# Attention units split into scores and softmax, with statistics kept twice, in a hybrid encoder on one core

## The chip, the cores and the metric

The kernel runs on one core of one Trainium2 chip. The metric is the device time of one execution in microseconds (us), as the median of several runs. Engines are named as the profile names them: PE (TensorE; PEld its weight loads), DVE (VectorE), ACT (ScalarE), POOL (GpSimd), SP (SyncE, which here issues DMAs); ACTq and SPq are the DMA issues of ACT and SP.

## The reference

Two layers of an encoder over 512 prompt frames and 64 sample frames (576 rows of 1024), with a half-step SwiGLU FFN before and after a mixing block. All is fp32.

```python
def layer(h, ...):
    h = ffn_half(h, n1, w1g, w1u, w1d)           # h + 1/2 * (silu(x@wg) * (x@wu)) @ wd, D_FF 2816
    z = rmsnorm(h, nm) @ w_in                    # 1824 columns: u, va | q, k, v | cq, ckv, kpe
    m, st = token_mix(z, ...)
    h = h + m @ w_out
    return ffn_half(h, n2, w2g, w2u, w2d), st
```

token_mix has three parts. A: `u * (W_s v + b)` in chunks of 128. B: sliding-window attention, 8 query heads on 2 key heads of 64, over the own 64-frame chunk and the 128 frames before it, with a learned sink per head in the softmax. C: latent attention of 4 heads, scores from a 64-wide and a 32-wide part over all keys so far, softmax, values from a 128-wide latent. Both softmaxes are

```python
    m = jnp.maximum(jnp.max(s, axis=-1, keepdims=True), sk)      # C: without the sink sk
    p = jnp.exp(s - m)
    den = jnp.sum(p, axis=-1, keepdims=True) + jnp.exp(sk - m)
    return jnp.einsum('...hgqk,...khd->...qhgd', (p / den).astype(v.dtype), v)
```

Keys and values (B), latent and rotated key (C) and va of the sample are stored as further outputs.

## The kernel before

An fp32 product is made of three fp32r matmuls: every weight and activation is split in a high part (ACT) and a low part (POOL or DVE), and high*high, high*low and low*high are added in PSUM. Activations lie transposed, 128 channels by 576 frames, as two halves of 288. Per layer come the first FFN, the mixing phase, the rest of the output projection (c_part, L1745), and the second FFN. Each engine runs its own program; they meet in semaphores.

The mixing phase is written by one table, PLAN (L166), a list of steps. Every engine walks it in order and issues what it has to do for a step, so the table sets the order on all of them at once: PE in L1595, ACT in L1195, DVE in L2361. A step `name@p` uses PSUM pair p (two banks, `ps[p]`); there are four pairs, and PE waits before a step until the last step in its pair has been emptied (`evacuated`, L263, `tensor_needs`, L292). The steps:

- `w:x`: ACT splits weight slot x (w_high, L846), POOL makes its low part (w_low, L793); raw weights come by SP's DMAs, two raw buffers and a ring of four split slots. z:k and z:v have theirs before the phase.
- `z:x`: one input projection, 48 matmuls (L1384); DVE empties it with the norm's scale (L2409). `sumx`, `sumkv`, `sumq`: sums of squares, with a Sqrt on ACT.
- `sw:x`, `rot:x`: rotary embedding of k and q0 to q3: ACT issues four DMAs that copy z with its halves swapped (L1225) into z_swapped, and DVE multiplies and adds (L2450, L2454, L2457). For kpe and qp the swap is a matmul (`rot32`). The two z_swapped buffers alternate over k, q0, q1, q2, q3.
- `tw`, `tc`, `tk`, `tv`, `tva`, `tckv`, `tkpe`, `rkv`, `rep`: transposes and copies. `a`: part A. `qp`, `qn`, `kn`, `vc`: projections of part C. `A:m` (12 matmuls) and `B:m` (24): the output projection of parts A and B, column tile m, added to h by DVE (L2539). The projection of part C is c_part.
- Part B has ten units (five tiles of 128 frames, the last of 64, by two head pairs): `S:n` scores and softmax, `T:n` the turn (transposes of the probabilities, L1713, copied out by ACT to probsT), `O:n` the product with the values (L1721). Part C has ten: `MS:n`, `MT:n`, `MO:n` (L1736), for tiles 1, 3, 4, 2, 0 with 256, 512, 320, 384 and 128 keys. Window units have 128 keys (S:0, S:1), 256 (S:2 to S:7) or 192 (S:8, S:9).

A step S is, over the engines: PE scores (L1692; MS L1699, L1704); DVE fill of masked columns (L2487, L2491), maximum (L2494), neg_max (L2499) and sink_arg (L2503); ACT exponential of the sink (L1293) and of the scores with their sums (L1295; MS L1303); DVE den_all (L2506), reciprocal (L2515), division (L2522, L2524; MS L2526). All this stands in one place of DVE's order:

```python
                            emit(nc.vector.tensor_tensor(by_group(sink_arg)[0:nq], by_group(neg_max)[0:nq], unit_sinks(sinks, jj)[0:nq], ALU.add), names[n])
                            n += 1
                            adid(f"{step}.4")
                            emit(nc.vector.tensor_tensor(den_all[0:nq, :], den[0:nq, :], sink_exp[0:nq, :], ALU.add), names[n])
```

`adid` is DVE's wait for ACT. There is one tile of each statistic and one of probs; probsT has two.

SP (L671 to L765) loads the slots in their order; between the slots B1 and B2 it waits for tk.1, tv.1, tkpe.1, tva:1.1 and tckv.1 and issues nine stores. Behind the low part of slot C1 it loads the first set of the second FFN (set_raw, L607), which ACT splits at L1133.

Of the kernel before, what the change touches and what calls it, by code (L numbers as in the profile page):

```python
# [22 lines left out]
F32 = mybir.dt.float32  # L23
# [142 lines left out]
PLAN = """w:q0 z:k@0 sumx@3 w:q1 z:v@1 sw:k tw@2 w:q2 z:q0@0 rot:k z:q1@1 sw:q0 w:q3 w:va0 w:va1 sw:q1 tc@2 w:u0 rot:q0  # L166
z:q2@3 sw:q2 rot:q1 z:q3@1 rot:q2 sw:q3 w:u1 z:va0@0 tk@2 w:ckv w:cq0 rot:q3 z:va1@3 tva:0@0 S:0@2 z:u0@3 tv@1
tva:1@0 a:0@3 T:0@1 S:1@2 z:u1@0 w:cq1 O:0@1 w:cq2 T:1@2 S:2@0 z:ckv@3 T:2@2 w:kpe S:3@3 z:cq0@1 O:1@0 sumkv@3
T:3@1 S:4@2 O:2@3 a:1@1 z:cq1@0 w:qn T:4@3 S:5@1 O:3@2 z:cq2@0 O:4@3 T:5@1 S:6@2 z:kpe@0 sumq@3 tckv@1 O:5@0
T:6@3 w:A0 rkv@1 S:7@2 rep@1 qp@3 vc:0@0 rot:kpe@1 T:7@0 S:8@3 w:A1 qn:0@2 O:6@1 A:0@0 kn:0@3 T:8@2 S:9@1 O:7@0  # L170
A:2@2 qn:1@3 w:B0 A:1@1 rot:qp@0 T:9@2 tkpe@1 O:8@3 O:9@2 A:4@1 MS:0@2 vc:1@1 kn:1@3 w:B1 A:3@2 A:7@3 MT:0@0 w:B2
MS:1@1 B:0@0 A:6@3 MT:1@2 A:5@0 MS:2@3 MO:0@1 B:1@2 B:2@0 MT:2@1 MS:3@2 MO:2@1 B:3@0 MO:1@3 MT:3@2 w:B3 MS:4@1
B:4@3 MO:3@2 MT:4@1 MS:5@0 B:5@1 MT:5@2 MS:6@3 B:6@0 w:C0 MO:4@1 w:C1 MT:6@2 MS:7@3 B:7@1 MO:5@3 MT:7@2 MS:8@0
MO:6@2 MT:8@0 MS:9@2 MO:8@1 MO:7@0 MT:9@2 MO:9@0""".split()
# [35 lines left out]
def scalar_ops(step):  # L210

    kind, arg = split(step)
    n = {"z": 0, "sumx": 1, "sumkv": 2, "sumq": 4, "tw": 1, "tv": 2, "tc": 2, "tk": 2, "tva": 2,
         "rkv": 2, "tkpe": 2, "rep": 1, "a": 1, "kn": 1, "S": 5, "O": 1, "MS": 2, "MO": 1}.get(kind, 0)
# [12 lines left out]

def vector_ops(step):
# [25 lines left out]
PE_STEPS = [s for s in MIX if s not in SLOT_ENDS and s in PAIRS]  # L254
ACT_STEPS = [x for s in MIX for x in scalar_ops(s)]
# [7 lines left out]
def evacuated(step):  # L263

    kind, arg = split(step)
    if kind in ("z", "qp", "qn", "O", "MO", "A", "B"):
        return "vector", f"{step}.0"
    if kind in ("rot", "a", "tckv"):
        return "vector", f"{step}.1"
    return "scalar", scalar_ops(step)[-1]  # L270


def buffer_of(step):

    kind, arg = split(step)
    turn = [s for s in MIX if split(s)[0] in ("T", "MT")]
    return turn.index({"T": "T", "O": "T", "MT": "MT", "MO": "MT"}[kind] + f":{arg}") % 2
# [14 lines left out]
def tensor_needs(step):  # L292
# [4 lines left out]
    if prior is not None:  # L297
# [29 lines left out]
        "T": lambda: [vector_ops(f"S:{arg}")[-1]],  # L327
        "MT": lambda: [vector_ops(f"MS:{arg}")[-1]],
# [15 lines left out]
def build(nc, a, outs):  # L344
    ctx = ExitStack()
    with ctx:
# [31 lines left out]
        eps = sb("eps", [P, 2])  # L378
# [4 lines left out]
        neg_max = sb("neg_max", [P, 4])  # L383
        sink_arg = sb("sink_arg", [P, 4])
        sink_exp = sb("sink_exp", [P, 4])
        den = sb("den", [P, 4])
# [79 lines left out]
        zr = [at("z_swapped0", [P, NT], F32, pT0_at + 5120), at("z_swapped1", [P, NT], F32, temp0 + U)]  # L466
# [372 lines left out]
        def _(act):  # L839
# [355 lines left out]
            def mixing(layer):  # L1195
# [18 lines left out]
                for step in MIX:  # L1214
# [20 lines left out]
                    if kind == "z":  # L1235
# [12 lines left out]
                        continue  # L1248
                    if kind == "a":
# [38 lines left out]
                    elif kind == "S":  # L1288
                        i, jj, t0, nq, keys = swa_unit(arg)
                        W = sum(n for _, n in keys)  # L1290
                        first = len(vector_ops(step)) - 7
                        dve_did(act, layer, f"{step}.{first + 2}")
                        emit(nc.scalar.activation(sink_exp[0:nq, :], sink_arg[0:nq, :], ACT.Exp), f"{step}.0")  # L1293
                        for j in range(B_GROUP):
                            emit(nc.scalar.activation(probs[0:nq, j * 256:j * 256 + W], flat(p)[0:nq, j * 256:j * 256 + W],  # L1295
                                                      ACT.Exp, bias=neg_max[0:nq, j:j + 1], scale=B_SCALE,
                                                      accum_out=den[0:nq, j:j + 1]), f"{step}.{1 + j}")
                    elif kind == "MS":
                        i, pair, t0, nq, keys = mla_unit(arg)
                        W = sum(n for _, n in keys)  # L1300
                        dve_did(act, layer, f"{step}.{len(vector_ops(step)) - 3}")
                        for j in range(2):
                            emit(nc.scalar.activation(probs[0:nq, j * 512:j * 512 + W], flat(p)[0:nq, j * 512:j * 512 + W],  # L1303
                                                      ACT.Exp, bias=neg_max[0:nq, j:j + 1], scale=q_scale[0:nq, i:i + 1],
                                                      accum_out=den[0:nq, j:j + 1]), f"{step}.{j}")
# [67 lines left out]
        def _(pe):  # L1373
# [221 lines left out]
            def mixing(layer):  # L1595
                s = ZIN
                for step in MIX:
# [52 lines left out]
                    elif kind == "rot":  # L1650
                        src = {"kpe": kpe_rep, "qp": zs[1]}[arg]
                        if arg == "kpe":
# [172 lines left out]
        def _(dve):  # L1825
# [535 lines left out]
            def mixing(layer):  # L2361
# [22 lines left out]
                for step in MIX:  # L2384
# [8 lines left out]
                    if kind not in ("sumx", "sumkv", "sumq", "tw", "rot"):  # L2393
# [46 lines left out]
                    elif kind == "rot":  # L2440
# [6 lines left out]
                        else:  # L2447
                            adid("rep.0")
                            dve.wait_ge(mix_in, layer * N_MIX_IN + N_MIX_IN)
# [28 lines left out]
                    elif kind in ("S", "MS"):  # L2478
# [17 lines left out]
                        n += 1  # L2496
                        if swa:

                            emit(nc.vector.scalar_tensor_tensor(out=by_group(neg_max)[0:nq], in0=by_group(top)[0:nq], scalar=-B_SCALE,  # L2499
                                                                in1=unit_sinks(neg_sink, jj)[0:nq], op0=ALU.mult, op1=ALU.min), names[n])  # L2500
                            own(names[n])
                            n += 1
                            emit(nc.vector.tensor_tensor(by_group(sink_arg)[0:nq], by_group(neg_max)[0:nq], unit_sinks(sinks, jj)[0:nq], ALU.add), names[n])  # L2503
                            n += 1
                            adid(f"{step}.4")
                            emit(nc.vector.tensor_tensor(den_all[0:nq, :], den[0:nq, :], sink_exp[0:nq, :], ALU.add), names[n])  # L2506
# [134 lines left out]
```

## Time and profile before

| | |
|---|---|
| runs, median (lowest to highest) | 2100.07 us (2094.56 to 2100.23), 3 runs |
| span of the profiled execution | 2090.4 us; its own time is one of the kind above, 4.2 to 9.8 us over the span |
| busy, share of the span | PE 98%, PEld 95%, DVE 80%, ACT 47%, POOL 17% |
| mean granted TensorE clock | 0.994 |
| DMA | 178.35 MB, mean 85 GB/s |

The span runs from the first to the last instruction. The page's busy time of PE is modelled at its ends, so 98% does not mean that it works at its peak all that time. The views used below are the page, the busy time by windows, the waits of one engine (who released it and how long it had been idle), and the timeline (start, duration, instruction, and in brackets the idle time before it with its releaser). Times in the timeline are us from the span's start.

### The profile page before, as it was taken

To read this page: it belongs to the slowest core of one execution; us is meant where nothing else is said; L and a number is where in the kernel's file an instruction comes from. 1 tells how busy PE (TensorE), PEld (TensorE's weight loads), DVE (VectorE), ACT (ScalarE), POOL (GpSimd) and SP (SyncE) were. 2 spreads that over 40 slices of the span, in tenths; PEclk is the share of its full clock that TensorE was granted. 3 is DMA by queue.
4 is the path that set the end of the run, shared out by engine and by line. 5 is a ranking of instruction groups with operands and counts; after the bars stand their busy time and mean duration, and the time that the engine had idled before them with its cause. 6 is when DMAs were issued, how large, how long until landed. Compare 5 with 4: busy or idle time off the path is not lost. (4 is left out here: it accounts for less than half of the span.)

```text
span 2090.4 us, 41116 instructions
## 1 busy us (share of the span) xinstructions
PE 2048.2 (98%) x15435; PEld 1978.9 (95%) x15435; DVE 1681.3 (80%) x2481; ACT 977.5 (47%) x1772; POOL 359.9 (17%) x219
## 2 busy tenths in 40 slices
PE   9999999999999999999999999999999899999998
PEld 7999999999778999999989999999987699999998
DVE  5999998655655999998889999975565579999975
ACT  6544453324535544463465654533344464444532
POOL 0322200141110222200023222002402112222000
PEclk9999999999999999999999999999999999999999
DMA  4223323351111233232223322325312023332231
GB/s 131 94 88 100 96 75 105 94 128 42 46 41 62 86 95 100 91 92 85 77 82 101 100 80 87 103 76 128 94 45 64 31 62 101 100 93 85 83 105 64
DMA packets 236727, 178.35 MB, mean 85 GB/s; under 512 B 35808, under 2 KB 231616, under 8 KB 236608
## 3 DMA queue, kind: packets, MB, share of 16 engines
q1 hardware_dynamic: 231712, 170.36, 27.4%
q10 hardware_dynamic: 4896, 6.36, 1.1%
q8 instruction: 80, 1.31, 0.3%
q14 instruction: 39, 0.32, 0.1%
HBM read 170.12 MB, written 3.62 MB: 83 GB/s over the span
## 5 line engine op out<-in xcount | busy, mean ns | idle before, releaser
L1437 PE MATMUL pair<-t_parts,chunk_high 128*128 128x288 f32 x4592 | 919.2, 296 | 5.2 <-POOL chunk_low L799 2.5
L1437 PEld LDWEIGHTS pair<-t_parts,chunk_high 128*128 128x128 f32 x4592 | 738.9, 189 | 6.6 <-POOL chunk_low L799 3.2
L1437 PE MATMUL pair<-t_parts,chunk_low 128*128 128x288 f32 x2296 | 678.9, 296 | 0.0
L1437 PEld LDWEIGHTS pair<-t_parts,chunk_low 128*128 128x128 f32 x2296 | 432.7, 188 | 0.0
L799 POOL TENSOR_TENSOR chunk_low<-set_raw,chunk_high 128x512 fp32r<-128x512 f32 x164 | 237.5, 1458 | 871.5 <-ACT chunk_high L898 871.5
L898 ACT ACTIVATE chunk_high<-chunk_sum 128x512 fp32r<-128x512 f32 x328 | 203.9, 631 | 373.4 <-DVE chunk_sum L1990 190.3
L2002 DVE TENSOR_TENSOR chunk_low<-chunk_sum,chunk_high 128x512 fp32r<-128x512 f32 x328 | 214.4, 694 | 9.2 <-ACT chunk_high L898 1.9
L793 POOL TENSOR_TENSOR w_low<-raw,w_high 128x1024 fp32r<-128x1024 f32 (+2 forms) x48 | 115.0, 2402 | 619.6 <-ACT w_high L846 619.6
L1384 PE MATMUL pair<-hidden_high,w_high 128*128 128x288 f32 x896 | 192.1, 296 | 0.0
L1384 PE MATMUL pair<-hidden_high,w_low 128*128 128x288 f32 x896 | 191.9, 296 | 0.0
L1384 PE MATMUL pair<-hidden_low,w_high 128*128 128x288 f32 x896 | 191.6, 296 | 0.0
L846 ACT ACTIVATE w_high<-raw 128x896 fp32r<-128x896 f32 (+2 forms) x112 | 110.1, 984 | 140.5 <-PE pair L1570 56.0
L898 ACT ACTIVATE chunk_high<-set_raw 128x512 fp32r<-128x512 f32 x246 | 149.3, 620 | 0.0
L1384 PEld LDWEIGHTS pair<-hidden_low,w_high 128*128 128x128 f32 x896 | 144.5, 189 | 0.0
L1384 PEld LDWEIGHTS pair<-hidden_high,w_high 128*128 128x128 f32 x896 | 144.2, 189 | 0.0
L1384 PEld LDWEIGHTS pair<-hidden_high,w_low 128*128 128x128 f32 x896 | 144.2, 189 | 0.0
L1384 PE MATMUL pair<-x_high,w_high 128*128 128x288 f32 x480 | 105.1, 300 | 0.0
L1384 PE MATMUL pair<-x_high,w_low 128*128 128x288 f32 x480 | 102.7, 296 | 0.0
L1384 PE MATMUL pair<-x_low,w_high 128*128 128x288 f32 x480 | 102.6, 295 | 0.0
L1985 DVE TENSOR_TENSOR chunk_sum<-set_raw 128x512 f32<-128x512 f32 x82 | 82.4, 1005 | 14.9 <-PE pair L1437 14.5
L1021 ACT ACTIVATE chunk_high<-chunk_sum 128x512 fp32r<-128x512 f32 x64 | 39.1, 633 | 110.5 <-DVE chunk_sum L1910 95.2
L926 ACT ACTIVATE outputs<-outputs 128x576 f32<-128x576 f32 x88 | 59.4, 686 | 59.9 <-DVE outputs L2071 59.6
(300 smaller groups left out, 3732.6 us busy)
## 6 DMA issues: line engine op xcount, KB each, us to landing
set_raw<-in_w_up_dram SPq DMA_DIRECT2D x44, 1024.0 KB, 5.3
set_raw<-in_w_gate_dram SPq DMA_DIRECT2D x44, 1024.0 KB, 5.3
raw<-in_w_down_dram SPq DMA_DIRECT2D x64, 448.0 KB, 3.8
down_raw<-in_w_down_dram SPq DMA_DIRECT2D x16, 1024.0 KB, 5.4
raw<-in_w_in_dram SPq DMA_DIRECT2D x20, 512.0 KB, 4.0
raw<-in_w_in_dram SPq DMA_DIRECT2D x16, 256.0 KB, 3.8
raw<-in_w_out_dram SPq DMA_DIRECT2D x8, 512.0 KB, 3.5
raw<-in_w_out_dram SPq DMA_DIRECT2D x16, 256.0 KB, 4.0
```

The source lines that it names most:

```text
L793: nc.gpsimd.tensor_tensor(**low_of(s, slot_size(s))).then_inc(low_ready, 1)
L799: nc.gpsimd.tensor_tensor(out=cl[:, j], in0=set_raw[b][:, :, int(j == A12), 0:P], in1=ch[:, j].bitcast(F32), op=ALU.subtract).then_inc(low ...
L846: nc.scalar.activation(wh[s % RING][:, 0:n], raw[s % RAW][:, raw_from(s):raw_from(s) + n], ACT.Copy).then_inc(high_ready, 1)
L898: nc.scalar.activation(ch[:, j], src, ACT.Copy).then_inc(chunk_high, 1)
L926: nc.scalar.activation(g, g, ACT.Silu).then_inc(silu_done, 1)
L1021: nc.scalar.activation(ch[:, down_unit(g, j)], src, ACT.Copy).then_inc(d_high, 1)
L1384: mm = nc.tensor.matmul(ps[p][:, half, 0:HALF], w, x[:, half * HALF:(half + 1) * HALF], start=first and k == 0 and q == 0, stop=last and k ...
L1437: mm = nc.tensor.matmul(out, c[:, j, p, :], tr[p // 2][:, seat(p), x, t, :], start=p == 0 and n == 0, stop=p == KP - 1 and n == 2)
L1985: ins = nc.vector.tensor_tensor(cf[:, S1], block(b, 0, 1), block(b, 1, 1), ALU.add)
L2002: nc.vector.tensor_tensor(cl[:, j], src, ch[:, j].bitcast(F32), ALU.subtract).then_inc(low_by_dve, 1)
```

## The change

Each attention unit becomes two steps of the plan: S (or MS) is scores, fill, maximum, neg_max and sink_arg; E (or ME) is the exponentials on ACT and sum, reciprocal and division on DVE. The pair of S counts as emptied with the last exponential of E. neg_max, sink_arg, sink_exp and den exist twice and alternate over the units, so that S of the next unit may stand before E of this one; probs stays one tile, and E of a unit stands behind the turn of the unit before. The plan has a new order and other pairs for nearly all steps. `ex:n` is an exponential of one element on ACT; `ex:0` stands ahead of the first unit, `ex:1` near the end. The swapped halves of k, q1 and q3 go to sq_tmp in place of a piece of probsT. The wait for the tables of rot:kpe and rot:qp stands at whichever comes first. What each instruction computes is unchanged.

```diff
-MO:6@2 MT:8@0 MS:9@2 MO:8@1 MO:7@0 MT:9@2 MO:9@0""".split()
+MS:8@0 ex:1 MT:7@1 ME:8 B:5@3 MO:6@0 MO:7@1 MS:9@3 MT:8@0 ME:9 B:4@2 MT:9@3 w:C0 B:6@0 MO:8@2 MO:9@3 B:7@1 w:C1""".split()
...
+    if kind in ("S", "MS"):
+        return "scalar", scalar_ops(step.replace("S:", "E:"))[-1]
...
-        "T": lambda: [vector_ops(f"S:{arg}")[-1]],
-        "MT": lambda: [vector_ops(f"MS:{arg}")[-1]],
+        "T": lambda: [vector_ops(f"E:{arg}")[-1]],
+        "MT": lambda: [vector_ops(f"ME:{arg}")[-1]],
...
-        neg_max = sb("neg_max", [P, 4])
+        neg_maxs = sb("neg_max", [P, 2, 4])
+        neg_max = [neg_maxs[:, b, :] for b in range(2)]
...
-        zr = [at("z_swapped0", [P, NT], F32, pT0_at + 5120), at("z_swapped1", [P, NT], F32, temp0 + U)]
+        zr = [sq_tmp, at("z_swapped1", [P, NT], F32, temp0 + U)]
...
+                    if kind == "ex":
+                        emit(nc.scalar.activation(first_exp, eps[:, 0:1], ACT.Exp), f"{step}.0")
+                        continue
+                    if kind == "E":
+                        i, jj, t0, nq, keys = swa_unit(arg)
+                        W = sum(n for _, n in keys)
+                        b, sc = parity(step), flat(PAIRS[scores_of(step)])
+                        dve_did(act, layer, vector_end(scores_of(step)))
+                        emit(nc.scalar.activation(sink_exp[b][0:nq, :], sink_arg[b][0:nq, :], ACT.Exp), f"{step}.0")
+                        for j in range(B_GROUP):
+                            emit(nc.scalar.activation(probs[0:nq, j * 256:j * 256 + W], sc[0:nq, j * 256:j * 256 + W],
+                                                      ACT.Exp, bias=neg_max[b][0:nq, j:j + 1], scale=B_SCALE,
+                                                      accum_out=den[b][0:nq, j:j + 1]), f"{step}.{1 + j}")
+                        continue
...
+                    elif kind in ("E", "ME"):
+                        swa = kind == "E"
+                        i, jj, t0, nq, keys = (swa_unit if swa else mla_unit)(arg)
+                        heads, wide = (4, 256) if swa else (2, 512)
+                        W = sum(n for _, n in keys)
+                        b, n = parity(step), 0
+                        adid(scalar_ops(step)[-1])
+                        total = den[b]
```

How the plan moves instructions, at the places the prediction speaks of. Names in the rows as above; numbers behind a name are buffers; the changed kernel's lines lie some 30 lower (L1747 is the turn, L1770 MO, L1733 and L1738 the scores MS, L1418 a product).

PE, the last units of the mixing phase of layer 0, before:

```order
L1736 MATMUL pair<-probsT_102,vc_tok 64x64 x6
L1713 MATMUL pair<-ident,probs 128x128 x6
L1699 MATMUL pair<-k_nopeT_132,q_nopeT_134 128x128 x2
L1704 MATMUL pair<-kpeT,q_peT 128x128 x2
L1736 MATMUL pair<-probsT_101,vc_tok 64x128 x6
L1713 MATMUL pair<-ident,probs 128x128 x2
L1699 MATMUL pair<-k_nopeT_133,q_nopeT_135 128x128 x2
L1704 MATMUL pair<-kpeT,q_peT 128x128 x2
```

And of the change, from MO:6 to the first rows of the product B:4:

```order
L1770 MATMUL pair<-probsT_101,vc_tok 64x128 x6
L1770 MATMUL pair<-probsT_102,vc_tok 64x128 x6
L1733 MATMUL pair<-k_nopeT_132,q_nopeT_134 128x128 x2
L1738 MATMUL pair<-kpeT,q_peT 128x128 x2
L1747 MATMUL pair<-ident,probs 128x128 x2
L1418 MATMUL pair<-mixed_high,w_high_51 128x288 x2
L1418 MATMUL pair<-mixed_low,w_high_51 128x288 x2
```

Before, the scores of MS:9 follow the turn of MT:8, and MT:9 follows with two MO steps between. Now MS:9 stands ahead of MT:8, and the product B:4 (24 matmuls) between MT:8 and MT:9.

ACT, the beginning of the phase of layer 0, from the Sqrt of the norm to the weights va1, before:

```order
L1256 ACTIVATE rms<-pair,eps 128x576
L846 ACTIVATE w_high_54<-raw_50 128x1024
L1225 DMA z_swapped_123<-z_90 32x576 x4
L1206 ACTIVATE w_sT<-pair 128x512
L846 ACTIVATE w_high_51<-raw_49 128x1024
L1225 DMA z_swapped_124<-z_91 32x576 x4
L846 ACTIVATE w_high_52<-raw_50 128x1024
L846 ACTIVATE w_high_53<-raw_49 128x1024
L846 ACTIVATE w_high_54<-raw_50 128x1024
```

And of the change, to the swaps of q0 and q2:

```order
L1253 DMA sq_tmp<-z_90 32x576 x4
L874 ACTIVATE w_high_53<-raw_49 128x1024
L1234 ACTIVATE cache_kT_ckvT<-pair 128x384
L1234 ACTIVATE cache_kpeT<-pair 128x256
L874 ACTIVATE w_high_54<-raw_50 128x1024
L1253 DMA z_swapped_123<-z_91 32x576 x4
L1278 ACT_TABLE_LOAD
L1278 ACTIVATE eps<-eps 128x1
L1253 DMA z_swapped_123<-z_91 32x576 x4
```

The first row is the swap of q1; the swap of q0, which came ahead of it, now follows behind two weight splits and two copies, and the table load has come ahead of the first unit.

DVE, the last two units, of the change (E rows are RECIPROCAL and the division under it; L2577 adds a product to h, L2574 is mixed_low):

```order
L2553 RECIPROCAL inv_den<-den 128x2
L2564 TENSOR_TENSOR probs<-probs,inv_den 128x2x128
L2577 TENSOR_TENSOR h<-pair,h 128x576
L2574 TENSOR_TENSOR mixed_low<-pair,mixed_high 128x128 x2
L2522 MEMSET pair 64x2x64
L2529 TENSOR_REDUCE top<-pair 128x2
L2539 TENSOR_SCALAR neg_max<-top,neg_q_scale 128x2
L2553 RECIPROCAL inv_den<-den 128x2
```

Before, fill, maximum, neg_max, reciprocal and division of a unit followed each other with the wait for ACT between; here ME:8 is over, and B:5, MO:6 and MO:7 lie between it and the fill of MS:9, whose division follows as ME:9.

## Rows read from the trace of the kernel before

**Rows 1.** The page, busy time and share of PE and its weight loads.
```profile
PE 2048.2 (98%) x15435; PEld 1978.9 (95%) x15435; DVE 1681.3 (80%) x2481; ACT 977.5 (47%) x1772; POOL 359.9 (17%) x219
```
**Rows 2.** Windows: both mixing phases, stretch, busy us (count), PEclk, DMA share, GB/s.
```profile
411.00:644.70 233.70, 222.28 (x1740) 194.75 (x1738) 132.13 (x234) 95.73 (x240) 52.64 (x22) 0.98 0.27 69
...
1439.80:1672.40 232.60, 220.31 (x1739) 193.43 (x1738) 131.38 (x234) 95.74 (x240) 52.80 (x22) 1.00 0.27 69
...
637.60:647.90 10.30, 7.94 (x44) 6.34 (x44) 2.82 (x9) 2.36 (x9) 0.00 (x0) 0.50 0.01 2
1671.90:1675.30 3.40, 2.94 (x12) 2.97 (x13) 0.83 (x2) 0.00 (x0) 0.00 (x0) 0.50 0.02 5
```
**Rows 3.** Waits of PE over the span: total us, times, longest.
```profile
PE pair L1713 <- DVE probs L2526: 10.5, 10, 2.0
PE pair L1713 <- issue: 4.0, 6, 1.1
```
**Rows 4.** Timeline of PE, end of mixing in layer 0: start, us.
```profile
637.20 0.41 PE L1713 MATMUL pair<-ident,probs 128*128 128x128 f32 x2 [1.97 <-DVE probs L2526]
...
641.97 0.66 PE L1713 MATMUL pair<-ident,probs 128*128 128x128 f32 x2 [1.00 <-DVE probs L2526]
643.11 0.69 PE L1736 MATMUL pair<-probsT,vc_tok 128*64 128x128 f32 x4 [0.47 <-ACT probsT L1206]
644.70 0.58 PE L1384 MATMUL pair<-mixed_high,w_high 128*128 128x288 f32 x1 [0.89 <-DVE mixed_low L2536]
```
**Rows 5.** Timeline, window unit S:5 on DVE, a copy on ACT, the turn on PE.
```profile
518.24 0.27 DVE L2487 MEMSET pair<- 64x256 f32 x1
...
522.71 0.16 DVE L2506 TENSOR_TENSOR den_all<-den,sink_exp 128x4 f32<-128x4 f32 x1 [2.15 <-ACT probs L1295]
...
523.73 0.68 DVE L2524 TENSOR_TENSOR probs<-probs,inv_den 128x512 f32<-128x512 f32 x1
...
517.23 1.00 ACT L1206 ACTIVATE probsT<-pair 128x1024 f32<-128x1024 f32 x1
...
524.51 1.06 PE L1713 MATMUL pair<-ident,probs 128*128 128x128 f32 x8 [1.10 <-issue]
```
**Rows 6.** Timeline of DVE, latent unit MS:8, fill and division.
```profile
634.47 0.17 DVE L2487 MEMSET pair<- 64x128 f32 x1 [0.91 <-PE pair L1704]
...
636.67 0.42 DVE L2526 TENSOR_TENSOR probs<-probs,inv_den 128x256 f32<-128x256 f32 x1
```
**Rows 7.** Timeline of PE, the product z:va0 and two transposes behind it.
```profile
451.32 0.43 PE L1384 MATMUL pair<-x_high,w_high 128*128 128x288 f32 x2
...
457.73 0.27 PE L1664 MATMUL pair<-ident,kT 128*128 128x128 f32 x1
457.83 0.27 PE L1665 MATMUL pair<-ident,kT 128*64 128x128 f32 x1
```
**Rows 8.** Swaps: timeline of ACT's issues; DMA issues with KB and us to landing.
```profile
424.02 2.53 ACTq L1225 DMA_DIRECT2D z_swapped<-z  x4
...
z_swapped<-z ACTq DMA_DIRECT2D x40, 72.0 KB, 2.8
```
**Rows 9.** Timeline of DVE and POOL near the rotation of q0.
```profile
432.65 0.76 DVE L2450 TENSOR_TENSOR kT<-z,cos 128x576 f32<-128x576 f32 x1
...
438.25 0.76 DVE L2409 TENSOR_TENSOR z<-pair,rms 128x576 f32<-128x576 f32 x1 [3.31 <-PE pair L1384]
439.04 2.65 DVE L2450 TENSOR_TENSOR qT<-z,cos 128x576 f32<-128x576 f32 x1
...
436.33 4.75 POOL L793 TENSOR_TENSOR w_low<-raw,w_high 128x1024 fp32r<-128x1024 f32 x2 [5.73 <-ACT w_high L846]
```
**Rows 10.** The first set of the second FFN: SP's issue, ACT's split, landing.
```profile
629.87 0.37 SPq L607 DMA_DIRECT2D set_raw<-in_w_up_dram  x1
...
654.25 1.04 ACT L1133 ACTIVATE chunk_high<-set_raw 128x1024 fp32r<-128x1024 f32 x1
...
set_raw<-in_w_up_dram SPq DMA_DIRECT2D x44, 1024.0 KB, 5.3
```

More of the change, by code:

```diff
@@ L254, with scores_of, parity @@
 PE_STEPS = [s for s in MIX if s not in SLOT_ENDS and s in PAIRS]
+SCORES = [s for s in MIX if split(s)[0] in ("S", "MS")]
+EXPS = [s for s in MIX if split(s)[0] in ("E", "ME")]
+TURNS = [s for s in MIX if split(s)[0] in ("T", "MT")]
+VALUES = [s.replace("T:", "O:") for s in TURNS]
+assert [s.replace("S:", "T:") for s in SCORES] == TURNS == [s.replace("ME:", "MT:") if s[0] == "M" else s.replace("E:", "T:") for s in EXPS]
+for n in range(len(TURNS)):
+    assert MIX.index(SCORES[n]) < MIX.index(EXPS[n]) < MIX.index(TURNS[n]) < MIX.index(VALUES[n])
+    if n + 1 < len(TURNS):
+        assert MIX.index(TURNS[n]) < MIX.index(EXPS[n + 1])
+    if n + 2 < len(TURNS):
+        assert MIX.index(EXPS[n]) < MIX.index(SCORES[n + 2]) and MIX.index(VALUES[n]) < MIX.index(TURNS[n + 2])
+def scores_of(step):
+    return step.replace("E:", "S:")
+def parity(step):
+    return SCORES.index(scores_of(step)) % 2
 ACT_STEPS = [x for s in MIX for x in scalar_ops(s)]
@@ L275, in buffer_of @@
     kind, arg = split(step)
-    turn = [s for s in MIX if split(s)[0] in ("T", "MT")]
-    return turn.index({"T": "T", "O": "T", "MT": "MT", "MO": "MT"}[kind] + f":{arg}") % 2
+    return TURNS.index({"T": "T", "O": "T", "MT": "MT", "MO": "MT"}[kind] + f":{arg}") % 2
 def before_in_pair(step):
@@ L1248, in mixing @@
                         continue
+                    if kind == "ex":
[12 more added lines that the diff above has]
+                        continue
+                    if kind == "ME":
+                        i, pair, t0, nq, keys = mla_unit(arg)
+                        W = sum(n for _, n in keys)
+                        b, sc = parity(step), flat(PAIRS[scores_of(step)])
+                        dve_did(act, layer, vector_end(scores_of(step)))
+                        for j in range(2):
+                            emit(nc.scalar.activation(probs[0:nq, j * 512:j * 512 + W], sc[0:nq, j * 512:j * 512 + W],
+                                                      ACT.Exp, bias=neg_max[b][0:nq, j:j + 1], scale=q_scale[0:nq, i:i + 1],
+                                                      accum_out=den[b][0:nq, j:j + 1]), f"{step}.{j}")
+                        continue
                     if kind == "a":
@@ L1287, in mixing @@
                         copy(knT[arg][:, :], flat(p)[:, 0:KEYS], f"{step}.0")
[L1288 to L1305, printed above, removed]
                     elif kind in ("T", "MT"):
@@ L1651, in mixing @@
                         src = {"kpe": kpe_rep, "qp": zs[1]}[arg]
-                        if arg == "kpe":
+                        if step == min(("rot:kpe", "rot:qp"), key=MIX.index):
                             pe.wait_ge(mix_in, layer * N_MIX_IN + N_MIX_IN)
@@ L2392, in mixing @@
                         own(DVE_STEPS[emitted[0] - 1])
[L2393 removed]
+                    if kind not in ("sumx", "sumkv", "sumq", "tw", "rot", "E", "ME"):
                         pe_did(dve, layer, step)
@@ L2448, in mixing @@
                             adid("rep.0")
+                        if step == min(("rot:kpe", "rot:qp"), key=MIX.index):
                             dve.wait_ge(mix_in, layer * N_MIX_IN + N_MIX_IN)
```

60 lines of the change are left out of this document (30 added, 30 removed).

## The prediction

> **What bounds the kernel.** The page comes first. TensorE (PE) is busy 2048.2 us of 2090.4 [rows 1], so a change of order can win only where PE is idle or slow. The three runs lie 4.2 to 9.8 us above that span (median 2100.07); I take the change off the median, since what lies outside the span is not touched. About 0.3% (6 us) is what a measurement of this kernel can tell from no change.
>
> The windows over the two mixing phases say how much there is: in layer 0, from 411.0 to 644.7, PE is busy 222.28 of 233.70 us; in layer 1 220.31 of 232.60 [rows 2]. That is 11.4 and 12.3 us idle, 23.7 of the span's 42.2. PE's waits name the releasers: the largest is the turn of the probabilities (L1713), which waits for the division (DVE, L2526) or for "issue", 10.5 and 4.0 us in all [rows 3]. The timeline shows where: the last units of latent attention have nothing between scores and turn, so PE stands 1.97 and 1.00 us, then 0.47 and 0.89 us before the output projection [rows 4]. DVE (132 us busy of 234), ACT and POOL are far from full [rows 2]. The bound inside this phase is latency: a chain PE, DVE, ACT, DVE, PE per unit, with too little PE work laid over it.
>
> **The change, term by term.**
>
> 1. *Idle taken away.* Before, a unit's step S held scores, statistics, exponentials and division, in one place of every engine's order, and one set of statistics allowed one unit in flight. Now S is scores and maximum, E the rest, and S of the next unit may be issued before E of this one has ended. What counts is PE work between the end of a unit's scores and its turn. The chain it must cover, for a window-attention unit of 256 keys: first fill at 518.24, sums added at 522.71, division over at 524.41, turn at 524.51; with the hand-over to the fill 6.5 us [rows 5]. The shortest latent one, 128 keys, has fill at 634.47 and division over at 637.09, so 2.8 us [rows 6]; wider ones lie between the two, some 3.5 us for 256 keys and 4.7 for 384 (estimates: the fill's row and these two chains, by the number of keys). PE work is priced by rows: a product of 48 matmuls is 6.4 us, from 451.32 to 457.73 [rows 7], so one of 24 is 3.2 to 3.4 and one of 12 is 1.6 to 1.8. Laying the new plan out with those and the durations of the small steps, I get from scores to turn 7.7 us or more for units S:0 to S:5, 6.9 and 6.8 at the shortest of the later ones (S:6, S:9), and for latent units 4.2 (MS:0, 256 keys), 4.8 (MS:5, 320 keys), 7.4 (MS:6) and 3.8 (MS:9, 128 keys). The order at the end shows it: a product of 24 stands between the last scores and their turn, where nothing stood. All cover their chains, by 0.3 to 10 us.
>
> The second chain is from turn to turn, because there is still one probs tile: transposes 1.06, copy out 1.00, exponentials (DVE waits 2.15 for them), sum and division 522.71 to 524.41, 6.1 us with the hand-overs [rows 5]. The shortest new distance of two window turns is 6.7 to 6.9 us (T:5 to T:6, T:8 to T:9, the latter with 192 keys); of two latent ones 3.7 (MT:8 to MT:9), where the chain is about 2.6 (128 keys: transposes 0.41, and the rest of rows 4 and 6 in place of rows 5). So the idle goes: -11.4 and -12.3 = **-23.7 us**.
>
> 2. *Tails.* Each pause also costs the drain that the view counts as busy: one matmul's record is 0.27 us where the next starts 0.10 later when nothing stops it [rows 7]. With some 19 pauses a layer at about 0.13 us: **-5 us** for both layers.
>
> 3. *The clock.* In 637.6 to 647.9 PE ran at a granted 0.50, the 1.2 GHz level, and in 1671.9 to 1675.3 again, while all other stretches of the phases show 1.00; both begin within or just behind the pauses of the last units [rows 2, 4]. Work of 7.94 and 2.94 us busy there would take half: **-5.4 us**. The Trainium skill says the same of the cause ("TensorE: Matmul & The Clock Gate", the section on oscillation: pauses of PE bring the gate back to half), and the trace agrees with it; nothing in the sum uses the page.
>
> Ceiling: 23.7 + 5 + 5.4 = 34 us.
>
> 4. *Pauses that the new order makes.* (a) Swaps. ACT now issues q1's half-swap ahead of q0's, with two weight splits (1.05 us each) and the table copies between. Four issues take 2.5 us and data land 2.8 us after issue [rows 8]. z:q1 is scaled at about 27.9 us of the phase, so q1's swap is issued by 30.5, q0's by 35.9 and landed at 38.7; rot:q0 ends at 40.3, and only then does DVE empty pair 0 (z:q2), which PE wants at 40.3 for tv: 1 us. (b) POOL. A DVE instruction with two SBUF inputs that meets a w_low waits for it: at 439.04 it took 2.65 us beside POOL's two w_low from 436.33 to 441.08 (2.4 each), against 0.76 at 432.65 without them, while the one that reads PSUM at 438.25 took its 0.76 beside the same POOL work [rows 9]. The Trainium skill has the rule ("GPSIMD Engine Reference", Specifications: contention with VectorE instructions in a two-port mode or with two SBUF inputs), and it speaks against this change, which lays those instructions more densely under 22 w_low a layer. I find three meetings where the cover is under 1 us: rot:q3 before S:1 (0.5), neg_max of S:3 with kpe's split, before T:3 (0.6), division of ME:6 with B3's split, before MT:6 (0 or 1.4; I take 0.7). (c) PSUM pairs that are emptied 0.4 to 0.8 us before they are needed, some 15 of them: 0.2. Sum 3.0 a layer, **+6 us**. Below, this is 0; above, each of four meetings costs a full w_low, 2.4 us, 9.6 a layer, 19 in all. I take 6 since only divisions and rotations that start inside a w_low pay.
>
> 5. *Covered, priced at nothing.* The statistics kept twice add no instruction. The extra exponential of one element brings the Exp table load ahead of the first unit, on ACT alone, where T:0 is covered by 12.9 us of products [rows 7]. q0's swap buffer is now sq_tmp, free from the first mean to cq0. The key copy tk and tkpe come later, and SP waits for them before nine stores and B2's weights: tkpe is copied at about 162.7 us of the phase, ten issues at 0.37 and a landing of 5.3 make 171.7 [rows 10], and ACT splits B2 at 177. If that cover went, B:4 would wait microsecond for microsecond. The last weight set C1 is split only behind MO:9: then w_low (2.4) and SP's load of the next FFN's first set, issued at 629.87 before, 14.8 us ahead of the projection. Now it is issued 0.7 us behind the projection's start and lands 5.3 later, at +6.0; ACT takes it at 654.25, +9.6 from 644.70, or about +8.2 at full clock [rows 4, 10]. 2 us are left. The FFNs stay as they are, PE-bound.
>
> Sum: -34 + 6 = **-28 us**, 2072.
>
> **Rivals.** *No new pause of note* (15%): -32 to -36, about 2066. For it: all worked slacks are positive but four. *Port and swaps bind* (19%): by the skill's rule taken strictly, every two-SBUF instruction in those four places meets a w_low whole: -34 + 19 = -15, 2085. Against it: before, with 22 w_low a layer, DVE lost no PE time that the waits show other than through L2526. *The FFN's first set is late* (6%): should w_low C1 slip behind others by 4 us, the load lands at +10, 2 us late, 4 in both layers: 2076. *The change does not do what it says* (3%): a pair is still given back only at the last exponential, so early scores could find none free and PE would pause as before: 2100. Against it: pairs are spread so that S of the next unit has another one than E. *Slower* (5%): E makes DVE stand waiting for ACT (2.15 us for a unit [rows 5]) with the emptying of z and B products behind it in its order. If PE then waits for a pair at each of the 20 turns, it decides once a turn costs more than 0.85 us (34 / 40); at 1.2 us a turn it is -34 + 48 = +14, 2114. Against it: I find the pair in hand at 18 of 20 turns.
>
> **How the numbers follow.** The forecast 2072 has 52% (2068 to 2079). With the rivals, 2062 to 2086 holds over eight tenths: below by the ceiling, above by the four full meetings. Faster by over 0.3%: 52 + 15 + 19 + 6 and a little less for the unforeseen, 0.89; within 0.3%: 0.06; slower 0.05.
>
> **What would show it.** Right: PE idle in each mixing phase near 3 us; the turn's waits on DVE below 2 us in both layers together; a granted clock of 1.00 through the phase and the projection; the phase 217.7 + 3 = 221 us. Term 4 right: PE waits at tv or the scores of S:0 on a DVE z or qT, and at T:3 and MT:6 on the division. Wrong: idle above 7 us a layer, a wait on a PSUM pair at many turns, or a wait for chunk_high at the first FFN tile.

## The result, and the profile after

The changed kernel takes 2058.0 us (median of 4 runs, 2057.43 to 2061.27) against 2097.6 for the kernel before (4 runs, 2094.56 to 2100.23): ratio 0.9816, 95% interval 0.9803 to 0.9828. It is faster by 39.6 us where I had forecast 28 off a median of 2100, so the time lies 14 us under the forecast and 4 under the lower end of the range.

The profiled executions differ by less than the medians: 2090.4 us of span before, 2059.5 now, 30.9 apart. On the page PE is busy 16.7 us less and idle 14.2 us less:

```profile
span 2059.5 us, 41110 instructions
...
PE 2031.5 (99%) x15435; PEld 1975.0 (96%) x15435; DVE 1683.0 (82%) x2481; ACT 978.1 (47%) x1776; POOL 359.7 (17%) x219
```

The instructions are the same but for ACT's one-element exponentials, two a layer; 42.2 us of PE idle [rows 1] have become 28.0. The windows of both kernels over each mixing phase with the output projection behind it (a little longer than in [rows 2], so that the last pause is inside) show where. Columns as in [rows 2]; first the kernel before:

```profile
411.00:659.10 248.10, 236.68 (x1836) 209.15 (x1835) 142.63 (x250) 102.74 (x251) 52.83 (x23) 0.98 0.27 69
1439.80:1686.40 246.60, 234.31 (x1836) 207.43 (x1835) 141.71 (x250) 102.75 (x251) 52.92 (x23) 0.99 0.27 70
```

and the changed kernel, with its two stretches at the granted 0.5 at the end:

```profile
412.00:645.10 233.10, 229.28 (x1837) 208.04 (x1836) 144.00 (x250) 103.04 (x253) 53.29 (x23) 0.99 0.28 74
1424.30:1655.40 231.10, 229.12 (x1837) 208.19 (x1836) 142.03 (x250) 103.24 (x253) 53.30 (x23) 0.99 0.29 74
472.40:475.80 3.40, 3.40 (x23) 3.14 (x20) 2.98 (x8) 2.06 (x11) 0.00 (x0) 0.50 0.03 8
1551.00:1554.40 3.40, 3.40 (x17) 3.30 (x17) 2.74 (x9) 2.12 (x5) 0.00 (x0) 0.51 0.00 0
```

494.7 us have become 464.2, 30.5 less: that is the whole difference of the spans but 0.4. PE stands 3.8 and 2.0 us where it stood 11.4 and 12.3. Its waits over the span now have three entries from these phases; the 10.5 us on the division of [rows 3] are gone, and nothing of [rows 4] is left at the phase's end (the last turns and outputs have no idle time before them, and ACT takes the next FFN's first set at 640.22, with the projection still running until 645.1):

```profile
PE pair L1726 <- DVE qT L2492: 3.5, 2, 2.4
...
PE pair L1696 <- DVE z L2443: 1.4, 2, 0.9
...
PE pair L1747 <- issue: 0.9, 2, 0.4
```

These are the scores of S:1 (2.40 and 1.07 us in the two layers), tv (0.94, 0.48) and the turn T:3 (0.43 each). PE's timeline in layer 0, where L1696 is tv and L1726 is S:1:

```profile
453.44 0.74 PE L1696 MATMUL pair<-ident,vT 128*128 128x128 f32 x5 [0.94 <-DVE z L2443]
...
471.42 2.04 PE L1726 MATMUL pair<-kT,qT 64*128 64x128 f32 x24 [2.40 <-DVE qT L2492]
```

And what DVE did on the way there: the rotation of q1 waits 3.56 us for its swap (4 issues begun at 440.05) and then takes 2.79 and 2.83 us, beside two of POOL's w_low. The rotation of q0 (450.12) begins as soon as that is over, with no wait for its own swap, and the emptying of z:q2, for which tv waits, comes behind it. The rotation of q3 takes 2.02 for an operation of 0.76:

```profile
444.44 2.79 DVE L2489 SCALAR_TENSOR_TENSOR sq_tmp<-sq_tmp,eps,sin 128x576 f32<-128x576 f32 x1 [3.56 <-DMA sq_tmp<-z]
447.26 2.83 DVE L2492 TENSOR_TENSOR qT<-qT,sq_tmp 128x576 f32<-128x576 f32 x1
450.12 0.76 DVE L2485 TENSOR_TENSOR qT<-z,cos 128x576 f32<-128x576 f32 x1
450.80 0.81 DVE L2489 SCALAR_TENSOR_TENSOR z_swapped<-z_swapped,eps,sin 128x576 f32<-128x576 f32 x1
...
452.53 1.55 DVE L2443 TENSOR_TENSOR z<-pair,rms 128x576 f32<-128x576 f32 x2
...
467.73 2.02 DVE L2485 TENSOR_TENSOR qT<-z,cos 128x576 f32<-128x576 f32 x1
...
470.51 0.76 DVE L2492 TENSOR_TENSOR qT<-qT,sq_tmp 128x576 f32<-128x576 f32 x1
```

POOL at the same times, the two w_low of 444.20 together in one row:

```profile
444.20 5.27 POOL L821 TENSOR_TENSOR w_low<-raw,w_high 128x1024 fp32r<-128x1024 f32 x2 [7.36 <-ACT w_high L874]
...
466.66 2.48 POOL L821 TENSOR_TENSOR w_low<-raw,w_high 128x1024 fp32r<-128x1024 f32 x1 [4.79 <-ACT w_high L874]
```

So the pauses went as forecast, and from profile to profile the gain is 30.9 against 28 forecast; the terms below show that part of this agreement is luck. Left to explain: the 9 us by which the medians differ more than the profiles, what each part of the change is worth, and which cause stands behind the pauses that are left.

### The profile page after: what moved, and what is told of

Read it like the earlier page. It is cut to its first block and busy times, and to the rows that moved or that the text cites. A ratio compares the mean times of both kernels' runs of the same rounds, so it can differ in the third digit from the quotient of the medians.

```text
span 2059.5 us, 41110 instructions
## 1 busy us (share of the span) xinstructions
PE 2031.5 (99%) x15435; PEld 1975.0 (96%) x15435; DVE 1683.0 (82%) x2481; ACT 978.1 (47%) x1776; POOL 359.7 (17%) x219
## 5 line engine op out<-in xcount | busy, mean ns | idle before, releaser
L1418 PE MATMUL pair<-hidden_high,w_high 128*128 128x288 f32 x896 | 191.9, 296 | 0.0
L1418 PE MATMUL pair<-hidden_high,w_low 128*128 128x288 f32 x896 | 191.9, 296 | 0.0
L1418 PE MATMUL pair<-hidden_low,w_high 128*128 128x288 f32 x896 | 191.8, 296 | 0.0
L1418 PEld LDWEIGHTS pair<-hidden_low,w_high 128*128 128x128 f32 x896 | 144.5, 189 | 0.0
L1418 PEld LDWEIGHTS pair<-hidden_high,w_high 128*128 128x128 f32 x896 | 144.2, 189 | 0.0
L1418 PEld LDWEIGHTS pair<-hidden_high,w_low 128*128 128x128 f32 x896 | 144.2, 189 | 0.0
L1418 PE MATMUL pair<-x_high,w_high 128*128 128x288 f32 x480 | 105.3, 301 | 0.0
L1418 PE MATMUL pair<-x_high,w_low 128*128 128x288 f32 x480 | 102.9, 296 | 0.0
L1418 PE MATMUL pair<-x_low,w_high 128*128 128x288 f32 x480 | 102.8, 296 | 0.0
```

The lines of the kernel that those rows point to most:

```text
L1418: mm = nc.tensor.matmul(ps[p][:, half, 0:HALF], w, x[:, half * HALF:(half + 1) * HALF], start=first and k == 0 and q == 0, stop=last and k ...
```

## Experiments

Every kernel here was timed in five rounds beside the kernel before. For each profile the time of both phases with their projections is split into three parts: idle (from PE's gaps), clock (half of PE's busy time inside stretches at 0.5), and rest, which is what is then left above the 454.5 us of e9, the kernel without pauses.

**e1_before.** The kernel before again, unchanged.

> The kernel before, unchanged, to settle the base of the sum. The profiled execution had a span of 2090.4 us and, with the 1.8 us that lie outside the span in the runs of the changed kernel, would read 2092.2, below all four runs shown (2094.56 to 2100.23). Theory: the executions differ in how long TensorE stands at the half clock. Then the runs' spans follow their granted clocks, about 2.1 us of span for each 0.001 of mean clock, a second profile shows other half-clock stretches than 637.6 to 647.9 and 1671.9 to 1675.3, with the same pauses. Rival: the pauses themselves vary (DMA landings); then the clocks are equal and the idle time of PE differs from 42.2 us by the difference of the spans.

Measured: 2096.7 us (11 runs, 2092.71 to 2099.55), ratio to itself 0.9998 [0.9989, 1.0007]; the profiled run has 2095.1 us of span, 4.7 more than the first profile. The windows of this profile:

```profile
411.70:662.70 251.00, 239.35 (x1837) 211.25 (x1836) 143.18 (x250) 102.83 (x251) 53.10 (x23) 0.97 0.26 68
1441.80:1691.10 249.30, 237.94 (x1837) 210.23 (x1836) 141.98 (x250) 102.87 (x251) 52.95 (x23) 0.97 0.26 69
536.70:540.10 3.40, 3.11 (x14) 2.05 (x15) 1.97 (x7) 1.16 (x5) 0.00 (x0) 0.50 0.13 43
639.10:652.80 13.70, 10.99 (x55) 9.10 (x56) 4.11 (x12) 3.33 (x11) 0.00 (x0) 0.50 0.03 5
1567.50:1570.90 3.40, 3.40 (x18) 2.62 (x14) 1.82 (x6) 1.02 (x5) 0.00 (x0) 0.50 0.00 0
1669.90:1680.20 10.30, 7.94 (x44) 6.35 (x45) 2.87 (x10) 2.32 (x9) 0.00 (x0) 0.50 0.01 2
```

The idle time is the same (23.0 us against 23.7), the pauses stand at the same places, but 30.8 us of the phases ran at the half clock instead of 13.7: 12.7 us of cost against 5.4. These 7.3 more, with idle 0.7 and rest 1.0 less, are the 5.6 by which these phases are longer. Over the 50 executions of this kernel in these series, the seven with the highest mean clock (0.993 and 0.994) have spans of 2090.4 to 2091.9, the four with the lowest (0.985) 2097.8 to 2098.2; between them the order is loose (at 0.987 spans run from 2092.4 to 2095.9). The slope is about a fifth of the 2.1 us for 0.001 that I had put down (some 0.45 by a line through 32 of them). A likely reason is that the mean counts stretches in which little work was slowed: the changed kernel's at its start, 8.2 to 25.3, costs at most 0.3 us (412.0 us to the mixing phase, 411.7 in e5, which has none there). Between these two profiles the cause is the clock; the slope was wrong, and over all executions the mean clock tells the span only loosely. The first profile of before had clock 0.994 and 2090.4 us, the lower end of those seven.

**e2_old_order.** The changed code with the order of before.

```diff
-... S:0@1 E:0 z:va0@3 rot:q3 z:va1@0 w:u1 T:0@3 tva:0@1 S:1@2 S:2@3 E:1 ...
+... tva:0@0 S:0@2 E:0 z:u0@3 tv@1 tva:1@0 a:0@3 T:0@1 S:1@2 E:1 z:u1@0 ...
```

> The changed code with the order of before: every entry for a unit's softmax stands directly behind that for its scores, the entries for the Exp table load are left out, pairs and swaps as before. Theory (the gain is all from the order): statistics kept twice and the moved swap scratch cost and give nothing, 2097 us, ratio 0.998 to 1.002, and PE idle again 11 to 12 us in each mixing phase. Rival (the code gives or takes something by itself, such as the scratch in another place or the table load): off by over 3 us.

Measured: 2096.3 us, ratio 0.9994 [0.9985, 1.0003]; idle 11.6 and 11.2 us. The code alone (statistics twice, two entries a unit, the swap scratch in sq_tmp) gives and takes nothing that these runs can tell (0.1%, 2 us). The gain is in the order, with the pairs that belong to it.

**e3_not_ahead.** The changed kernel, one unit in flight.

```diff
-... S:1@2 S:2@3 E:1 tva:1@1 w:ckv z:u0@0 w:cq0 T:1@1 E:2 ...
+... S:1@2 E:1 tva:1@1 w:ckv z:u0@0 w:cq0 T:1@1 S:2@3 E:2 ...
```

> The changed kernel, but each unit's scores moved to directly before its softmax, behind the turn of the unit before: one unit in flight again; order of everything else, pairs and swaps as changed. Theory (half of the idle goes through scores ahead, half through more work laid between): by my layout of the order the cover falls below the chain at S:6 (2.2 of 6.5 us), S:7 (3.7), S:8 and S:9 (4.9), MS:1 (2.2), MS:3 (1.6) and MS:5 (2.6), about 12 us of pauses a layer: 2080 us. Rival (the new order of products alone does it, scores ahead is an ornament): 2058 to 2062. Second rival (without scores ahead the new order is worse than the old, since products stand between softmax and turn no better): 2095 or more.

Measured: 2138.9 us, ratio 1.020 [1.0186, 1.0213]: the second rival (2095 or more), and far above even that bound. The phases take 270.2 and 267.5 us with 26.5 and 23.8 of idle and 30.7 at half clock in each. PE's waits name what all three had left out:

```profile
PE pair L1418 <- ACT probs L1297: 12.3, 6, 2.6
PE pair L1683 <- ACT probs L1287: 6.9, 2, 3.4
PE pair L1770 <- ACT probs L1297: 6.7, 4, 2.6
```

A product or an output (L1418, L1770) finds its PSUM pair still held by a unit's exponentials. A pair that holds scores is busy until the last exponential; moved later, the scores give it back later, while the step that takes it next is where it was.

**e6_pairs.** e3 with the pairs dealt out anew (for instance z:q0@3, z:q3@0, S:0@2, T:0@1, S:1@3, in place of 0, 2, 1, 3, 2).

> As e3_not_ahead (2139), each unit's scores directly before its softmax, but with the PSUM pairs dealt out anew: each step takes the pair that by my layout comes free first. Theory (in e3 the pairs of the changed kernel, laid out for early scores, are held by the exponentials when the next step wants them: 16 of its 26.5 us of pauses in layer 0 end on ACT's exponentials): these waits fall under 4 us a layer, the turns' waits stay at some 8 to 12 us a layer, and the clock recovers: 2085 to 2100. Rival (one unit in flight is what costs, whatever the pairs): above 2120.

Measured: 2121.1 us, ratio 1.0113 [1.0098, 1.0129]. The waits on the exponentials are gone, 18 us of the median with them (11.4 us of the phases in the two profiles, of which e3's was its fastest execution and e6's its slowest), but the turns stand 26.5 us, both layers together:

```profile
PE pair L1747 <- DVE probs L2564: 13.5, 6, 3.7
PE pair L1747 <- DVE probs L2562: 8.1, 2, 4.2
PE pair L1747 <- issue: 3.9, 4, 1.0
PE pair L1747 <- DVE mixed_low L2569: 1.0, 2, 0.5
```

Idle 20.4 and 20.0 us, 64.8 us at the half clock. My sum of 12 us of pauses a layer was too low, and the rival named there (one unit in flight costs) holds for the two dealings of pairs tried: the new order of products is 24 us worse than the old one if scores aren't ahead.

**e10_old_ahead.** The other half: the old order (- is e2's), scores one place up, pairs dealt out by the same rule as in e6.

```diff
-... T:4@3 S:5@1 E:5 O:3@2 z:cq2@0 O:4@3 T:5@1 S:6@2 E:6 ...
+... S:5@0 T:4@2 E:5 O:3@1 z:cq2@3 O:4@2 S:6@1 T:5@0 E:6 ...
```

> The changed code with the order of before (e2_old_order, 2096.3), but each unit's scores moved one place up, ahead of the turn of the unit before it (18 of 20 units), and the pairs dealt out to the one that comes free first. Theory (scores ahead is the lever; the scores' own 0.3 to 2 us and the turn's 0.4 to 1 us are laid over each chain): pauses before turns fall from 11.4 to 3 or 4 us a layer, those at the last two latent units stay (2.9 and 2.2 us of work over a chain of 2.8), clock stretches become few: 2068 to 2078. Rival (the gain needs the products laid out anew as well): 2085 or more. Second rival (pairs bind): PE's waits on ACT's exponentials above 5 us a layer, 2090 or more.

Measured: 2081.6 us (2081.33 to 2082.59), ratio 0.994 [0.9926, 0.9954], between the theory and its rival. Idle 7.2 and 7.0 us, part of it at the last latent units with their outputs and the projection; half clock for 6.8 and 10.2 us. Scores ahead by one place are worth some 15 us in the old order (2096.3 to 2081.6; 11 by the ratios, since the kernel before was 3.6 us faster in this series; 15.9 by the phases of the profiles, 499.8 to 483.9). The other 23 (22.2 by the phases, to e5's 461.7) need the products laid between. Neither half does it by itself.

**e4_swaps.** q0's swap and rotation ahead of z:q1.

```diff
-... z:q0@0 tw@2 z:q1@1 w:q3 sw:q1 rot:q1 w:va0 tc@2 w:va1 sw:q0 ex:0 rot:q0 z:q2@0 ...
+... z:q0@0 tw@2 sw:q0 rot:q0 z:q1@1 w:q3 sw:q1 rot:q1 w:va0 tc@2 w:va1 ex:0 z:q2@0 ...
```

> The changed kernel with q0's half-swap and rotation moved ahead of z:q1 and q1's (between the copy of w_sT and z:q1). Theory (the pauses at tv and before S:1 come from q1's swap being issued ahead of q0's, and the half-clock stretch behind the S:1 pause from that pause): pauses 0.94 and 2.40 in layer 0 and 0.48 and 1.07 in layer 1 shrink to at most 0.5 each, the stretch at half clock near 472.4 goes: about 2058 - 6 = 2052 us. Rival (POOL's w_low beside the rotations causes the S:1 pause): the pause at tv goes, that before S:1 stays above 1.5 us in layer 0: 2056.

Measured: 2055.2 us (2054.87 to 2056.34), ratio 0.98 [0.9786, 0.9813]. The pauses at tv and the half-clock stretch behind S:1 are gone; the pause before S:1 is 1.32 and 0.88. So the place of q0's swap and rotation, which the edit moves together, made 1.1 us of the 2.4 in layer 0 and 0.2 of the 1.1 in layer 1, and something else the rest.

**e5_after.** The changed kernel again.

> The changed kernel, unchanged, beside the others of this series. Theory (what is above the sum of the changed kernel's profiled execution is its 17.1 us stretch at half clock near the start, 8.2 to 25.3): the other executions lack it and have spans near 2056; median 2057.5 to 2058.5. A second profile shows the same pauses (0.9 and 0.5 at tv, 2.4 and 1.1 before S:1, 0.4 at T:3 in each layer), and the mixing phase with its projection at 231 to 233 us. Rival (the start's stretch is common): half of the executions above 2060.

Measured: 2058.3 us (2056.97 to 2060.35), ratio 0.9815 [0.9802, 0.9829]; one execution of five above 2060. Profile: span 2056.7, phases 232.2 and 229.5, the same pauses with 1.9 before S:1, half clock at 471.6 to 475.1 in the mixing phases and nowhere else in them. The median is the one expected, but the reason given for it does not hold: of the five executions the one with mean clock 0.993 has a span of 2055.5 and one with 0.998 has 2058.6, so a low mean clock does not mark the slow ones.

**e7_swaps_u1.** e4, with one weight split later.

```diff
-... rot:q3 z:va1@0 w:u1 T:0@3 tva:0@1 S:1@2 ...
+... rot:q3 z:va1@0 T:0@3 tva:0@1 w:u1 S:1@2 ...
```

> As e4_swaps (2055.2), with ACT's split of u1's weights, and so POOL's w_low of it, moved behind the copies of va_tok. In e4 the multiplication of z by cos for q3 took 2.05 us beside that w_low, and PE stood 1.32 us before S:1 for q3's rotation. Theory (the contention with POOL makes that pause): the multiplication takes 0.76 again, the pause before S:1 is at most 0.1 us in layer 0 and in layer 1: about 2053. Rival (the rotation is late because DVE serves E:0 and z:va0 first): the multiplication is shorter but the pause stays above 0.8 us.

Measured: 2054.2 us (2052.22 to 2054.53), and no pause left before S:1 in either layer. The same DVE instruction as in after's view above, in this kernel's timeline, with POOL idle from 458.7 to 469.61:

```profile
465.39 0.76 DVE L2485 TENSOR_TENSOR qT<-z,cos 128x576 f32<-128x576 f32 x1
```

The contention is shown: 2.05 us in e4 with POOL at work beside it, 0.76 without, and PE's pause goes with the difference. It has only moved: the w_low that starts at 469.61 now meets neg_max of S:1, which takes 2.27 us for 0.16, and no pause of PE follows.

```profile
469.75 2.27 DVE L2534 SCALAR_TENSOR_TENSOR neg_max<-top,neg_sink 128x4 f32<-128x4 f32 x1
```

**e8_best.** e4 with q3's rotation ahead of E:0 and w:kpe behind T:3 (u1's split not moved).

```diff
-... S:0@1 E:0 z:va0@3 rot:q3 z:va1@0 ...
+... S:0@1 rot:q3 E:0 z:va0@3 z:va1@0 ...
-... z:ckv@0 w:kpe S:3@3 S:4@1 E:3 z:cq0@0 T:3@3 sumkv@2 ...
+... z:ckv@0 S:3@3 S:4@1 E:3 z:cq0@0 T:3@3 w:kpe sumkv@2 ...
```

> As e4_swaps, with q3's rotation put ahead of the first unit's softmax, and kpe's weight split put behind T:3. Theory: S:1's pause (1.32 and 0.88) goes whatever POOL does at that time; neg_max of S:3 takes 0.16 us instead of 1.28 and T:3's pause (0.43 in each layer) goes; the turn T:0 has 12.9 us of products over it and stays in time. No PE pause above 0.2 us is left in the mixing phases: 3.1 us of pauses and some tails off 2055.2: about 2051.5, the lowest of all. Rival (a pause moves to T:0 or to z:va1): 2054 to 2056.

Measured: 2054.4 us; the rival. S:1's and T:3's pauses are gone, and a new one of 1.43 and 0.96 us stands at T:0, on DVE's z. The division of S:0, now where q3's rotation was, met the w_low that starts at 463.58:

```profile
463.68 2.57 DVE L2560 TENSOR_TENSOR probs<-probs,inv_den 128x256 f32<-128x256 f32 x1
```

It takes 0.43 elsewhere. Here the reordering of DVE only chose who pays; in e7 and e9 POOL's instruction moved instead, to where the work over it was enough.

**e9_final.** e7 and w:kpe behind T:3 together.

> e7_swaps_u1 (2054.2) with kpe's weight split put behind T:3, q3's rotation where it was. Theory: the two things proven apart add: no pause before S:1 (e7) and none at T:3, where neg_max of S:3 takes 0.16 us instead of 1.28: 0.43 us and a tail a layer, 2053.2, about 1 us below e7, which is near what five rounds can tell; PE idle in both mixing phases together under 0.3 us. Rival (the split meets another instruction at its new place and the pause moves to T:4 or sumkv): 2054 to 2055.

Measured: **2052.0 us** (2051.39 to 2052.80), ratio 0.9799 [0.9786, 0.9813] to the kernel before, whose median in this series was 2093.7, with five of nine executions at mean clock 0.993 or 0.994. Its spans, 2049.6 to 2051.0, lie below all those of the changed kernel (2055.2 to 2059.5): some 6 us faster than it by the medians, 3.5 by the ratios (the kernel before was 3.7 us faster in this series), and 7.2 by the phases of the two profiles (454.5 against e5's 461.7). The windows:

```profile
411.80:639.10 227.30, 227.29 (x1836) 206.69 (x1835) 144.75 (x250) 103.27 (x253) 52.73 (x23) 1.00 0.29 75
1418.30:1645.50 227.20, 227.20 (x1837) 206.65 (x1836) 143.99 (x250) 103.27 (x253) 53.17 (x23) 1.00 0.29 75
```

PE is busy in all of 227.3 and 227.2 us, at the full clock. neg_max of S:3 takes 0.16 us, against 1.28 in the changed kernel beside POOL's w_low of 1.57:

```profile
502.57 1.28 DVE L2534 SCALAR_TENSOR_TENSOR neg_max<-top,neg_sink 128x4 f32<-128x4 f32 x1
...
502.27 1.57 POOL L821 TENSOR_TENSOR w_low<-raw,w_high 128x640 fp32r<-128x640 f32 x1 [8.97 <-ACT w_high L874]
```

With no pause and no half clock left, these phases are the measure for the sum.

## Why the prediction was wrong, step by step

Both phases with projection, us (idle from the gaps, clock and rest as said above the experiments):

| | length | idle | clock | rest |
|---|---|---|---|---|
| before, first profile | 494.7 | 23.7 | 5.4 | 11.1 |
| before, e1 | 500.3 | 23.0 | 12.7 | 10.1 |
| after | 464.2 | 5.8 | 3.4 | 0.5 |
| after, e5 | 461.7 | 5.1 | 1.7 | 0.4 |
| e9 | 454.5 | 0.0 | 0 | 0 |

**The base** is the step that failed: "I take the change off the median, since what lies outside the span is not touched." What lies outside the span is 1.8 us (2061.27 against 2059.5 in the changed kernel's profiled run); the first profile of before would so be an execution of 2092.2. The other 2 to 8 us up to its shown runs were inside their spans. Those runs left no profile; in e1's, a slower execution, the time more is in these very phases, as half clock that the change takes away. So the change was priced in one of the fastest executions and taken off a median of slower ones. Between two executions near their medians, e1 (2095.1) and e5 (2056.7), it is 38.4 us: idle 23.0 to 5.1, clock 12.7 to 1.7, rest 10.1 to 0.4.

**Term 1, idle, -23.7:** right. All of it went (e9 shows that none has to stay), the mixing phases took 220.6 and 220.3 us against 221 forecast, and every cover that I had worked out for turns from S:0 to MS:9 but T:3's held. The rival "a pair is still given back only at the last exponential" described a true limit; e3 shows what it costs where the pairs do not fit.

**Term 2, tails, -5:** mis-sized, and its cause only in part the one named. What went is 11.1 and 10.1 us in two profiles, with 37 and 36 pauses of over 0.05 us: 0.3 for each where I took 0.13 from the ends of two matmuls. But the rest does not follow the pauses. With the new order of products it is 6.0 us in e3, with 43 pauses, and 4.4 in e6, with 26; with the old order it is 8.5 in e10, with 20. So a part of it, several us, belongs to the old order of PE's steps and not to its pauses; by what means stays open.

**Term 3, clock, -5.4:** right as a reading of the execution profiled, and short for one near the median, where the phases lose 12.7 us to it and get 11.0 back (e1 to e5). "A granted clock of 1.00 through the phase" was wrong too: each phase of the first profile of after has one stretch, 3.4 us of cost in all, that I had priced at nothing.

By terms, from e1 to e5: idle -17.9 (forecast -23.7 + 6 = -17.7), clock -11.0 (-5.4), rest -9.7 (-5): -38.6 in place of -28. Against the first profile of before the right sum was -23.7 - 11.1 - 5.4 + 9.7 (5.8, 3.4 and 0.5, what after has left) = -30.5, which is what the windows show: tails priced 6.1 too low and a clock that was not all given back nearly cancel in it, and that is luck.

The 14 us by which the time lies under 2072 are then: 2.5 because the median of three runs (2100.1) stood above that of four (2097.6), 5.6 of clock, 4.7 of rest, 0.2 of idle, and 1.0 between these two profiles and the medians.

**Term 4, new pauses, +6:** 5.8 us of idle, the sum right and its parts not. (a) tv stood 0.94 and 0.48 (1.0 forecast), on DVE's z as named, but by another path than I had worked out. q0's swap, issued by 445.67 and landed some 2.1 later, had landed some 2 us before DVE came to q0's rotation at 450.12; DVE was held by q1's rotation, of which the two w_low of 444.20 made 5.62 us out of some 1.6. This is the largest meeting with POOL, 4 us, and it was not on my list, so the size forecast for tv is luck; no run took POOL away there alone. The delay also carries on to q3's rotation (e4). (b) S:1 2.40 and 1.07 instead of 0.5; T:3 0.43 each instead of 0.6; MT:6 nothing instead of 0.7. The Trainium skill's rule on POOL beside a DVE instruction with two SBUF inputs ("GPSIMD Engine Reference", Specifications) agrees with the trace at each of the three places tried: e7 (2.05 to 0.76 us), e9 (1.28 to 0.16) and, against my expectation, e8 (0.43 to 2.57). (c) No pair cost anything.

**Term 5, covered:** held. e2 shows that the code, without the one-element exponentials, costs nothing by itself, and the FFN's first set was taken 5 us before the projection ended.

Of the rivals, "no new pause of note" (2066) was nearest in time and wrong in cause: the new pauses came as forecast.

Not settled: why the half clock comes in one execution and not in another of the same program with the same pauses, and what makes the stretch at 1551.0 in after (1544.6 in e7, 1545.8 in e8), where PE is busy throughout, in small matmuls, and no pause stands before it; e5 and e9 don't have it. What makes up the rest beyond the ends of matmuls before a pause was not tried by itself.

## What to carry to other kernels

Before you take a change off a median, ask to which of the executions your profile belongs: compare its span and mean granted clock with those of the runs, and where the stage that you change holds half-clock stretches, price them from two profiles. In a pipeline of PE, DVE and ACT, issuing early, the products laid between and the PSUM pairs are one decision: of the gain of 39 us, scores ahead alone gave some 15, the new order of products alone lost 24, and pairs that did not fit cost 18 more. Where a DVE instruction between SBUF tiles is late, look at POOL beside it before you reorder DVE, and move POOL's instruction to where PE has work laid over it.

## What the runs showed of the hardware

- Pauses of PE can cost more than their length. Here 23 us of idle went together with 5 to 13 us lost to the half clock and 10 to 11 us of further busy time, of which the pauses explain only a part (e3: 50 us of idle, 6.0 of rest); in e6 40 us of idle came with 64.8 us at the half clock. Taking away tv's pause and 1.1 us of the one before S:1 (e4) also took the stretch at the granted 0.5 behind it (472.4 to 475.8; in e5 again, 471.6 to 475.1). That pauses bring the half clock is also what the Trainium skill says ("TensorE: Matmul & The Clock Gate", the section on a second failure mode: with short idle times between groups of matmuls the clock goes back and forth between its two levels); the stretch at 1551.0, with PE busy in 3.40 of its 3.40 us, is one that no pause in this trace explains.
- The half clock differs between executions of one program: 13.7 and 30.8 us in the mixing phases of two profiles of the kernel before, at nearly equal idle time (23.7 and 23.0 us).
- Contention with POOL also stretches the smallest DVE instructions: 128x4 elements took 1.28 us instead of 0.16 beside a w_low of 1.57, and 2.27 beside one of 2.39 (e7).
